# A two-layer decoder with top-2 experts on one core: sums of x kept in PSUM, two more weight slots, other load order

## Chip, cores, metric

One core of one Trainium2 chip. The metric is the device time of one execution in microseconds (us). The kernel before takes 749.85 us, the median of 3 runs (747.26 to 752.99).

## What is computed

Two decoder layers over 256 tokens of width 1024, in fp32, batch 1. The reference, cut to what matters here:

```python
for l in range(2):
    h = rms_norm(x, norm1_g[l])
    proj = h @ w_in[l]                       # 1024 x 3072
    o_da = diff_attention(...)               # 4 heads of 2 x 64
    o_sb = stick_breaking_attention(...)     # 8 heads of 64
    x = x + concat(norm(o_da), norm(o_sb)) @ w_out[l]
    h2 = rms_norm(x, norm2_g[l])
    # 32 experts in 4 groups: best group, then the best 2 of its 8 experts, with weights w
    hg = einsum('sd,edf->sef', h2, w_gate)   # every expert: 1024 x 256
    hu = einsum('sd,edf->sef', h2, w_up)     # 1024 x 256
    act = silu(hg) * hu * combine
    x = x + einsum('sef,efd->sd', act, w_down)   # 256 x 1024
```

Only the two chosen experts of a token count, so the kernel computes each expert on its own tokens alone. All weights are read once: 96 matrices of 1024 KB for the experts of a layer, and 16 such pieces for its two projections (12 of `w_in`, 4 of `w_out`).

## The kernel before

The five engines each run their own program, written out by hand, and meet by semaphores. One layer has three stretches. First comes attention: x is transposed (`transpose_x`, line 1162), projected block by block, the heads are computed, and `out_proj` adds to x. Then comes routing: the router's matmuls (`router`, L1304), a long row of small DVE operations that finds the experts, the ranks of tokens within an expert and the counts, and the selection matrices. `keep_clock` (L1311) issues matmuls whose result nobody reads.

Then come the experts, in 8 sets of 4 experts ("lanes"). A set gives each of its experts 32 slots for tokens; a fixed pair of sets comes first (sets 0 and 1), and the other six are sorted by how many tokens their fullest expert has. Where an expert has more than 32 tokens, the set makes further rounds (`more`, as against `first`). In this run the third set of each layer does. A set's work on PE, in order, is:

- `gate_or_up` twice (L1353): the gate and the up product, 4 experts side by side in the array, each reading its weights from slots of SBUF;
- `gather` of the *following* set (L1328): its tokens' normed x, picked by a matmul with a 0/1 matrix; then the transposition of its selection weights (`transpose_weights`, L1337);
- `transpose_act` (L1374), then `down` in two column halves (L1385), which ends with the signal that SP takes as `dn_used`;
- `scatter` (L1397): four matmuls that bring the rows back to tokens, into four banks of PSUM, from where DVE adds each to `x_sb` (`into_x`, L904).

Beside it ACT computes the exponential of the gate (L595) and copies half of y (L599); DVE finishes the activation (L876 to L887), copies it (L892), copies the other half of y (L896) and makes the following set's selection.

**Weights and slots.** SBUF holds 19 slots of 1024 KB for weights. Gates and ups use alternate slots by the parity of the set, but lane 3's up has a single slot (9) for both parities, and the four downs have one set of slots. So before routing ends, 19 matrices of a layer can be there: all 12 of set 0, and 4 gates and 3 ups of set 1. SP issues all loads into one queue, in program order, and an issue that waits holds back all behind it (`load_first_sets`, `load_further_sets`). For each set g from 1 to 7 the latter issues, in this order: up of lane 3 of set g once the ups of set g-1 are used; the four gates of g+1 once the gates of g-1 are used (`gate_used`, raised by ACT after its exponential, L612 and L625); the four downs of g once those of g-1 are used (`dn_used`, L638); three ups of g+1. For g = 1 the gates come ahead of the up. In set 7 the downs come as 8 half matrices, so that the first column half can start early. The numbers of the six sorted sets are read into registers in one go (L415), once the whole sort is done (`routed`).

PE reads a set's count (how full its fullest expert is) after `transpose_act` of the set before it, and for set 0 after it has waited for `routed`. The first set's gathered tokens are copied by DVE after the sort.

Of the kernel before, what the change touches and what calls it, by code (L numbers as in the profile page):

```python
# [24 lines left out]
ALU = mybir.AluOpType  # L25
# [3 lines left out]
P = 128  # L29
# [62 lines left out]
SC_BANK = [(4, 5), (6, 7)]  # L92
# [28 lines left out]
def decoder(nc, const, x, norm1_g, w_in, q_norm_g, k_norm_g, lambda_q1, lambda_k1, lambda_q2, lambda_k2,  # L121
            da_out_g, sb_out_g, w_out, norm2_g, w_router_group, b_router_group, w_router_expert,
            b_router_expert, w_gate, w_up, w_down, out):
    with ExitStack() as ctx:
# [9 lines left out]
        xn = sb("xn", [P, TT, D])  # L134
        hTbuf = sb("hTbuf", [P, KC * SEQ])
        qkT = sb("qkT", [P, 4 * PAIRS * SEQ])
        cst = sb("cst", [P, C_END])
        g1T = sb("g1T", [P, KC])
        g2T = sb("g2T", [P, KC])
        wr = sb("wr", [P, KC, GROUPS + EXPERTS])  # L140
# [50 lines left out]
        hT = hTbuf[:, :].rearrange("p (k t) -> p k t", k=KC)  # L191

        def slot(n):
            return wbuf[:, n * SLOT:(n + 1) * SLOT]
        stage = slot(SLOT_STAGE).rearrange("p (b t c) -> p b t c", b=2, t=TT)
# [5 lines left out]
        sp = [xn[:, w // 2, (w % 2) * HALF:(w % 2 + 1) * HALF] for w in range(4)] + \  # L202
# [8 lines left out]
        def take(n):  # L211
# [4 lines left out]
        eg, rg, tg = take(FF), take(FF), take(FF)  # L216
        act_sb = take(FF)
        actT = take(FF).rearrange("p (c s) -> p c s", c=FC)
        sel = take(TT * P).rearrange("p (t s) -> p t s", t=TT)
        selw = take(TT * P).rearrange("p (t s) -> p t s", t=TT)  # L220
        selwT2 = [take(TT * P).rearrange("p (t s) -> p t s", t=TT),
                  hTbuf[:, KC * P:KC * P + TT * P].rearrange("p (t s) -> p t s", t=TT)]
        hgT_more = hTbuf[:, 0:KC * P].rearrange("p (k s) -> p k s", k=KC)
        selwT_more, sel_more, selw_more = [hTbuf[:, (KC + n * TT) * P:(KC + (n + 1) * TT) * P]
                                           .rearrange("p (t s) -> p t s", t=TT) for n in (1, 2, 3)]

        y_more = hTbuf[:, 0:D]
        actT_more = hTbuf[:, (KC + 2 * TT) * P:(KC + 3 * TT) * P].rearrange("p (c s) -> p c s", c=FC)
        act_more = hTbuf[:, (KC + 3 * TT) * P:(KC + 4 * TT) * P]
# [4 lines left out]
        first_half, more_half = slice(0, FF), slice(FF, 2 * FF)  # L234
        SELW_BANK = 6
        FIRST_GATE, FIRST_UP, MORE_GU = 2, 3, 5
        FIRST_ACT, MORE_ACT = 7, 4
        FIRST_DN, MORE_DN = (4, 5), (2, 3)
# [11 lines left out]
        dn_in, last_dn_in = sem("dn_in"), sem("last_dn_in")  # L250
        out_done = sem("out_done")
# [18 lines left out]
        pos_ps, total_ps, routed = sem("pos_ps"), sem("total_ps"), sem("routed")  # L270

        STEPS = ["sel_ready", "selw_ready", "gathered0", "gathered1", "selwT_ps", "hg0", "hg1", "selwT_out", "gu_ps", "gate_exp",
                 "act_out", "actT_ps", "actT_out", "dn0_ps", "dn1_ps", "y_d", "y_a", "sc00_ps", "sc01_ps", "sc10_ps", "sc11_ps"]
        first = {n: sem(n) for n in STEPS}
        more = {n: sem("more_" + n) for n in STEPS}
        x_more, x_moe, x_tile = sem("x_more"), sem("x_moe"), [sem(f"x_tile{t}") for t in range(TT)]
# [16 lines left out]
        def params(l):  # L293
            yield dag[:, :], bcast(da_out_g[l], 2 * HD)
            yield sbg[:, :], bcast(sb_out_g[l], HD)
            yield g2T[:, :], norm2_g[l].rearrange("(p k) -> p k", k=KC)
            yield wr[:, :, 0:GROUPS], w_router_group[l].rearrange("(p k) n -> p k n", k=KC)
            yield wr[:, :, GROUPS:], w_router_expert[l].rearrange("(p k) n -> p k n", k=KC)
            yield br[:, 0:GROUPS], bcast(b_router_group[l], GROUPS)
            yield br[:, GROUPS:], bcast(b_router_expert[l], EXPERTS)  # L300
        N_PAR = 7 * 16
# [1255 lines left out]
```

## Time and profile before

| | |
|---|---|
| timed runs, median (range) | 749.85 us (747.26 to 752.99) |
| the profiled execution | 746.18 us |
| its span, first to last instruction | 744.4 us |
| mean granted TensorE clock | 0.956 |
| PE busy | 656.6 us (88%) |
| DVE, ACT busy | 309.4 us, 117.9 us |
| moved from and to HBM | 239.13 MB, 321 GB/s over the span |

The profile counts times in us from the first instruction. The experts' stretch of the first layer runs from about 167 to 378 us, that of the second from about 534 to 741 us. A busy share over the whole span mixes the stretches, so the readings below go by stretch.

### The profile page before, as it was taken

To read this page: it belongs to the slowest core of one execution; us is meant where nothing else is said; L and a number is where in the kernel's file an instruction comes from. 1 tells how busy PE (TensorE), PEld (TensorE's weight loads), DVE (VectorE), ACT (ScalarE), POOL (GpSimd) and SP (SyncE) were. 2 spreads that over 40 slices of the span, in tenths; PEclk is the share of its full clock that TensorE was granted. 3 is DMA by queue.
4 is the path that set the end of the run, shared out by engine and by line. 5 is a ranking of instruction groups with operands and counts; after the bars stand their busy time and mean duration, and the time that the engine had idled before them with its cause. 6 is when DMAs were issued, how large, how long until landed. Compare 5 with 4: busy or idle time off the path is not lost.

```text
span 744.4 us, 12442 instructions
## 1 busy us (share of the span) xinstructions
PE 656.6 (88%) x4804; PEld 379.6 (51%) x4805; DVE 309.4 (42%) x633; ACT 117.9 (16%) x288; POOL 8.5 (1%) x18
## 2 busy tenths in 40 slices
PE   7999999988798898775999999999888989885866
PEld 4478555475455354423344875555744545533522
DVE  0445664153334343422333476631634344422413
ACT  3103442220000000000031035313100000000000
POOL 0002000000000000000020000000000000000000
PEclk8999999999899999978999999999999999988979
DMA  8798436537999999999999631394299999999995
GB/s 312 257 355 280 168 113 273 227 123 284 381 422 395 392 424 421 421 421 423 383 360 390 278 144 66 114 390 163 77 397 421 422 422 421 422 422 421 422 402 222
DMA packets 52920, 239.13 MB, mean 321 GB/s; under 512 B 7761, under 2 KB 8049, under 8 KB 29329
## 3 DMA queue, kind: packets, MB, share of 16 engines
q1 hardware_dynamic: 52416, 238.16, 80.3%
q0 software_dynamic: 464, 0.47, 0.5%
q8 instruction: 23, 0.38, 0.2%
q14 instruction: 17, 0.13, 0.0%
HBM read 237.56 MB, written 1.05 MB: 321 GB/s over the span
## 4 chain that ended last, share of the span: by engine, by line
PE 67%; DMA 18%; DVE 6%; issue 5%; DVEq 2%; SPq 1%; ACT 1%; ACTq 0%
DMA wbuf<-in_w_down 17%; PE bank L1199 13%; PE bank L1385 11%; PE bank L1353 8%; PE bank L1189 7%; PE bank L1297 7%; PE bank L1397 6%; PE bank L1328 5%; PE bank L1364 2%; DMA wbuf<-in_w_in 1%; PE bank L1277 1%; SPq L366 1%; PE bank L1258 1%; PE bank L1304 1%; PE bank L1232 1%
## 5 line engine op out<-in xcount | busy, mean ns | idle before, releaser
L1199 PE MATMUL bank<-wbuf,hTbuf 128*128 128x512 f32 x256 | 115.8, 608 | 3.7 <-DMA wbuf<-in_w_in 3.4
L1385 PE MATMUL bank<-wbuf,qkT 128*32 128x512 f32 x512 | 71.6, 708 | 52.9 <-DMA wbuf<-in_w_down 45.7
L1353 PE MATMUL bank<-wbuf,qkT 128*32 128x256 f32 x2048 | 113.8, 380 | 2.2 <-DVE qkT L868 2.2
L1353 PEld LDWEIGHTS bank<-wbuf,qkT 128*32 128x32 f32 x2048 | 65.3, 110 | 54.2 <-issue 10.6
L1199 PEld LDWEIGHTS bank<-wbuf,hTbuf 128*128 128x128 f32 x256 | 48.8, 194 | 62.9 <-issue 59.2
L1328 PE MATMUL bank<-qkT,xn 128*128 128x128 f32 x512 | 64.6, 286 | 11.6 <-issue 10.7
L1328 PEld LDWEIGHTS bank<-qkT,xn 128*128 128x128 f32 x512 | 61.3, 199 | 18.9 <-issue 18.9
L904 DVE TENSOR_TENSOR x_sb<-x_sb,bank 128x512 f32<-128x512 f32 x72 | 49.5, 688 | 50.8 <-PE bank L1397 50.8
L1385 PEld LDWEIGHTS bank<-wbuf,qkT 128*32 128x32 f32 x512 | 17.2, 127 | 97.4 <-issue 90.4
L1189 PE MATMUL bank<-hTbuf,wbuf 128*128 128x256 f32 x256 | 56.5, 380 | 0.0
L1297 PE MATMUL bank<-wbuf,hTbuf 128*128 128x512 f32 x128 | 56.0, 593 | 0.0
L1189 PEld LDWEIGHTS bank<-hTbuf,wbuf 128*128 128x128 f32 x256 | 48.2, 190 | 7.0 <-issue 0.7
L896 DVE COPY qkT<-bank 128x512 f32<-128x512 f32 x16 | 11.1, 692 | 76.2 <-PE bank L1385 76.2
L1297 PEld LDWEIGHTS bank<-wbuf,hTbuf 128*128 128x128 f32 x128 | 23.9, 190 | 27.7 <-issue 27.7
L878 DVE RECIPROCAL qkT<-qkT 128x256 f32<-128x256 f32 x18 | 31.6, 1753 | 1.4
L1397 PE MATMUL bank<-qkT 128*128 128x512 f32 x64 | 30.1, 612 | 2.3 <-DVEq L957 2.3
L599 ACT COPY qkT<-bank 128x512 f32<-128x512 f32 x16 | 9.4, 586 | 132.9 <-PE bank L1385 132.9
L1397 PE MATMUL bank<-qkT,hTbuf 128*128 128x512 f32 x64 | 30.3, 616 | 0.0
L892 DVE COPY qkT<-bank 128x256 f32<-128x256 f32 x16 | 6.8, 424 | 55.6 <-PE bank L1374 55.6
L595 ACT ACTIVATE qkT<-bank 128x256 f32<-128x256 f32 x18 | 6.9, 385 | 127.0 <-PE bank L1353 113.2
L1397 PEld LDWEIGHTS bank<-qkT 128*128 128x128 f32 x64 | 11.0, 189 | 21.7 <-issue 17.9
L1041 DVE TENSOR_TENSOR x_sb<-x_sb,bank 128x512 f32<-128x512 f32 x8 | 5.5, 685 | 37.3 <-PE bank L1297 37.3
(219 smaller groups left out, 589.4 us busy)
## 6 DMA issues: line engine op xcount, KB each, us to landing
wbuf<-in_w_gate SPq DMA_DIRECT2D x64, 1024.0 KB, 14.3
wbuf<-in_w_up SPq DMA_DIRECT2D x64, 1024.0 KB, 17.9
wbuf<-in_w_down SPq DMA_DIRECT2D x56, 1024.0 KB, 13.4
wbuf<-in_w_in SPq DMA_DIRECT2D x24, 1024.0 KB, 14.6
wbuf<-in_w_out SPq DMA_DIRECT2D x8, 1024.0 KB, 6.4
wbuf<-in_w_down SPq DMA_DIRECT2D x16, 512.0 KB, 7.4
x_sb<-in_x SPq DMA_DIRECT2D x2, 512.0 KB, 5.9
out<-x_sb SPq DMA_DIRECT2D x2, 512.0 KB, 2.6
```

Source lines behind the costliest of these rows:

```text
L599: nc.scalar.copy(dst[:, HALF:], ps[bank][:, :]).then_inc(s["y_a"], 1)
L878: V.reciprocal(rg, rg)
L896: V.tensor_copy(dst[:, 0:HALF], ps[bank][:, :]).then_inc(s["y_d"], 1)
L904: last.append(V.tensor_tensor(x_sb[:, t, c], x_sb[:, t, c], ps[SC_BANK[t][h]][:, :], ALU.add))
L1189: last = MM(ps[PROJ_BANK[i][t]][:, a * SEQ:(a + 1) * SEQ], block_rows(i, k)[:, cols], hT[:, k, :], start=(k == 0), stop=(k == KC - 1))
L1199: last = MM(ps[PROJ_BANK[i][t]][:, :], hT[:, k, t * P:(t + 1) * P], block_rows(i, k), start=(k == 0), stop=(k == KC - 1))
L1297: last = MM(ps[OP_BANK[t][h]][:, :], hT[:, k, t * P:(t + 1) * P], block_rows(i, k), start=(k == 0), stop=(k == KC - 1))
L1328: last = MM(ps[k // 4][:, (k % 4) * P:(k % 4 + 1) * P], xn[:, t, k * P:(k + 1) * P], sel[:, t, :], start=(t == 0), stop=(t == TT - 1))
L1353: last = MM(ps[bank][j * SLOTS:(j + 1) * SLOTS, 0:FF], hgT[:, k, j * SLOTS:(j + 1) * SLOTS], halves[:, at[j], k, :], start=(k == 0), stop= ...
L1364: last = MM(ps[MORE_GU][j * SLOTS:(j + 1) * SLOTS, :].rearrange("p (a f) -> p a f", a=2), hgT_more[:, k, j * SLOTS:(j + 1) * SLOTS], halve ...
L1385: last = MM(ps[banks[h]][j * SLOTS:(j + 1) * SLOTS, :], src[:, c, j * SLOTS:(j + 1) * SLOTS], at[j][:, c * D + h * HALF:c * D + (h + 1) * ...
L1397: MM(ps[SC_BANK[t][h]][:, :], weights[:, t, :], src[:, h * HALF:(h + 1) * HALF], start=True, stop=True).then_inc(s[f"sc{t}{h}_ps"], 1)
```

## The change

It does six things.

1. **Slots.** The buffers `xn` (normed x and attention output) and `hTbuf` (x transposed) become two more weight slots, 19 (`SLOT_XN`) and 20 (`SLOT_HT`). Lane 3's up of odd sets goes to slot 19, lane 0's down of odd sets to slot 20. So 21 matrices are loaded ahead: `up(1,3)` after the attention output is transposed, and `down(1,0)` after the router's matmuls.
2. **Load order.** For g from 1 to 7 SP now issues: four gates of g+1, four ups of g+1, downs of lanes 1 to 3 of g, down of lane 0 of g+1. Set 7 has 6 half matrices at the end.
3. **x in PSUM.** After the router, `keep_x` writes x by four matmuls with the identity into banks 4 to 7; every scatter adds to them there, and x is copied out once at the end of the layer, three quarters by DVE and one by ACT. `into_x` goes. The normed x, which the gathers read, is written by ACT to a scratch tile and then, by a second copy (`normed_to_x`), in place of x.
4. **Order within a set.** With four banks taken, downs of both kinds share banks 2 and 3. The selection weights of a set are transposed after its own ups, no longer ahead of its downs. In the last set the scatters of the first column half stand between the two halves of the downs.
5. **Counts and numbers.** SP reads each set's number just ahead of its gates. PE reads the count of the next set after the ups of a set; for set 0 it waits for `first_counts`, an earlier signal than `routed`. ACT raises `gate_used` ahead of its exponential. DVE copies the first half of set 0's gathered tokens before the sort, and ACT the second.
6. **Router by column halves.** The router's rows and the transposes of x for it go by column halves, so that a half can be transposed when its half of x is there.

```diff
-SLOTS_W = 19
-SLOT_STAGE, SLOT_VALUES, SLOT_SCRATCH = 13, 14, 15
+SLOTS_W = 21
+SLOT_STAGE, SLOT_VALUES, SLOT_SCRATCH, SLOT_XN, SLOT_HT = 13, 14, 15, 19, 20
-UP_SLOT = [[4, 5, SLOT_STAGE, 9], [6, 7, 8, 9]]
-DOWN_SLOT = [10, 11, SLOT_VALUES, 16]
+UP_SLOT = [[4, 5, SLOT_STAGE, 9], [6, 7, 8, SLOT_XN]]
+DOWN_SLOT = [[10, 11, SLOT_VALUES, 16], [SLOT_HT, 11, SLOT_VALUES, 16]]
...
+                sp_.wait_ge(oT_ps, l * 4 + 4)
+                load_up(l, 1, 3)
                 sp_.wait_ge(oproj_ps, l * 4 + 3)
                 load_gate(l, 1, 3)
...
+                sp_.wait_ge(lg_ps, (l + 1) * TT)
+                load_down(l, 1, 0)
 
             def load_further_sets(l):
                 sp_.wait_ge(routed, l + 1)
-                for g in range(2, SETS):
-                    at = SETS - g
-                    kept = sp_.value_load(which[0:1, at:at + 1], min_val=int(BIG) - SETS + 1, max_val=int(BIG) - 2)
-                    set_at[g] = sp_.snap(int(BIG) - kept)
                 for g in range(1, SETS):
-
-                    if g > 1:
-                        sp_.wait_ge(up_used, l * SETS + g)
-                        load_up(l, g, LANES - 1)
                     if g + 1 < SETS:
+                        at = SETS - (g + 1)
+                        kept = sp_.value_load(which[0:1, at:at + 1], min_val=int(BIG) - SETS + 1, max_val=int(BIG) - 2)
+                        set_at[g + 1] = sp_.snap(int(BIG) - kept)
                         sp_.wait_ge(gate_used, l * SETS + g)
                         for j in range(LANES):
                             load_gate(l, g + 1, j)
-                    if g == 1:
                         sp_.wait_ge(up_used, l * SETS + g)
-                        load_up(l, g, LANES - 1)
+                        for j in range(LANES):
+                            load_up(l, g + 1, j)
                     sp_.wait_ge(dn_used, l * SETS + g)
                     if g + 1 < SETS:
-                        for j in range(LANES):
+                        for j in range(1, LANES):
                             load_down(l, g, j)
-                        for j in range(LANES - 1):
-                            load_up(l, g + 1, j)
+                        load_down(l, g + 1, 0)
                     else:
                         for h in range(2):
-                            for j in range(LANES):
+                            for j in range(1, LANES):
                                 load_down_half(l, g, j, h)
...
+            def normed_to_x(l, t):
+
+                act.wait_ge(x_kept, l * TT + t + 1)
+                nc.scalar.copy(xn[:, t, :, :], xn_first[t]).then_inc(xn_ready, 1)
...
+                with act.If(most <= SLOTS):
+                    act.wait_ge(first["gu_ps"], act.snap(n * LANES))
+                    act.sem_inc(gate_used, 1)
                 gate(first, n, FIRST_GATE)
-
                 with act.If(most <= SLOTS):
-                    act.sem_inc(gate_used, 1)
                     act.wait_ge(up_ps, act.snap(n * LANES))
                     act.sem_inc(up_used, 1)
+                weights_copy(first, n, selwT, SELW_BANK)
...
-                for t, add in enumerate(into_x(first, n)):
-                    add.then_inc(x_tile[t], 1)
-                gap().then_inc(x_moe, 1)
...
+                for t, h in ((0, 0), (1, 0), (0, 1)):
+                    dve.wait_ge(x_ps[t][h], l + 1)
+                    V.tensor_copy(x_sb[:, t, h * HALF:(h + 1) * HALF], ps[X_BANK[t][h]][:, :]).then_inc(x_tile[t], 1)
...
+            def keep_x(t):
+
+                for h in range(2):
+                    last = MM(ps[X_BANK[t][h]][:, :], ident, x_sb[:, t, h * HALF:(h + 1) * HALF], start=True, stop=False)
+                last.then_inc(x_kept, 1)
...
+            def downs_and_scatters(s, n, parity, src, weights, second_half, last=False):
+
                 pe.wait_ge(s["actT_out"], n)
...
+                pe.wait_ge(s["selwT_out"], n)
+                down(s, n, parity, src, 0)
+                if last:
+                    scatter(s, n, weights, 0, last)
+                down(s, n, parity, src, 1, second_half)
+                if not last:
+                    scatter(s, n, weights, 0, last)
+                scatter(s, n, weights, 1, last)
...
                 gate_or_up(n, FIRST_UP, UP_SLOT[parity], up_ps)
+
+                pe.wait_ge(routed, l + 1)
+                pe.reg_mov(count, pe.value_load(cnt[0:1, bass.ds(SETS - 1 - g, 1)], min_val=0, max_val=SEQ))
+                transpose_weights(first, n, SELW_BANK)
```

Where instructions move, at three places. The first is the end of SP's queue of expert loads, from the last gate of set 7 to the first issue group of set 7's halves. Before:

```order
L359 ISA
L359 DMA wbuf<-in_w_gate 128x2048
L366 DMA wbuf<-in_w_down 128x2048 [waits dn_used]
L366 DMA wbuf<-in_w_down 128x2048 x3
L363 DMA wbuf<-in_w_up 128x2048 x3
L363 DMA wbuf<-in_w_up 128x2048 [waits up_used]
L370 DMA wbuf<-in_w_down 128x2x512 [waits dn_used]
L370 DMA wbuf<-in_w_down 128x2x512 x3
```

And now, from the same gate on:

```order
L362 ISA
L362 DMA wbuf<-in_w_gate 128x2048
L366 DMA wbuf<-in_w_up 128x2048 [waits up_used]
L366 DMA wbuf<-in_w_up 128x2048 x3
L370 DMA wbuf<-in_w_down 128x2048 [waits dn_used]
L370 DMA wbuf<-in_w_down 128x2048 x3
L375 DMA wbuf<-in_w_down 128x2x512 [waits dn_used]
L375 DMA wbuf<-in_w_down 128x2x512 x2
```

The four ups of set 7 moved from behind the downs of set 6 to ahead of them; behind those three downs there is now one down of set 7, and then the halves.

The second is PE within an even set, from the gather of the following set to the point ahead of the downs. Before (`actT` in `qkT`, the `cst` operand is the identity):

```order
L1325 REGISTER_ALU
L1328 MATMUL bank<-qkT,xn 128x128 [waits sel_ready]
L1328 MATMUL bank<-qkT,xn 128x128 x15
L1337 MATMUL bank<-cst,qkT 128x128 [waits selw_ready,selwT_out,x_moe]
L1337 MATMUL bank<-cst,qkT 128x128
L1374 MATMUL bank<-cst,qkT 128x128 [waits act_out]
L1374 MATMUL bank<-cst,qkT 128x128
L1446 ISA
L1446 TENSOR_LOAD sorted_i
L1446 ISA x3
L1448 COMPARE_AND_BRANCH [waits dn_in]
```

Now the same reading of the count (`TENSOR_LOAD`) and the transposition of the weights (L1365) follow the last up matmuls (L1381):

```order
L1381 MATMUL bank<-wbuf,qkT 32x256 x15
L1473 ISA [waits routed]
L1473 TENSOR_LOAD sorted_i
L1473 ISA x2
L1365 MATMUL bank<-cst,qkT 128x128 [waits selw_ready]
L1365 MATMUL bank<-cst,qkT 128x128
L1475 COMPARE_AND_BRANCH
```

The reading moved from ahead of the downs to between the ups and the gather, where PE's next matmuls stand behind it.

The third is PE in the last set, the downs (L1385, now L1411) and what follows. Before:

```order
L1385 MATMUL bank<-wbuf,qkT 32x512 [waits actT_out]
L1385 MATMUL bank<-wbuf,qkT 32x512 x7
L1382 ISA
L1385 MATMUL bank<-wbuf,qkT 32x512 [waits last_dn_in]
L1385 MATMUL bank<-wbuf,qkT 32x512 x7
L1453 COMPARE_AND_BRANCH
```

Now, with the scatters (L1419) in between and behind:

```order
L1411 MATMUL bank<-wbuf,qkT 32x512 [waits selwT_out,actT_out]
L1411 MATMUL bank<-wbuf,qkT 32x512 x7
L1419 MATMUL bank<-qkT 128x512 [waits y_d]
L1419 MATMUL bank<-qkT 128x512
L1411 MATMUL bank<-wbuf,qkT 32x512 [waits last_dn_in]
L1411 MATMUL bank<-wbuf,qkT 32x512 x7
L1419 MATMUL bank<-qkT 128x512 [waits y_a]
L1419 MATMUL bank<-qkT 128x512
```

Each pair of scatters now stands directly behind the half of the downs whose result it needs.

## Rows read from the trace of the kernel before

**Rows 1.** The page: DMA busy tenths and GB/s in 40 slices of 18.6 us.

```profile
DMA  8798436537999999999999631394299999999995
GB/s 312 257 355 280 168 113 273 227 123 284 381 422 395 392 424 421 421 421 423 383 360 390 278 144 66 114 390 163 77 397 421 422 422 421 422 422 421 422 402 222
```

**Rows 2.** Chain that ended last: start us, us, what.

```profile
328.87 22.05 DMA wbuf<-in_w_down
350.91 0.30 issue
351.21 6.37 PE bank L1385 x32
357.58 3.72 PE bank L1397 x8
361.30 7.17 PE bank L1353 x128
...
370.50 3.85 PE bank L1385 x32
374.35 3.72 PE bank L1397 x8
378.07 0.90 PE bank L1162 x8
...
714.54 5.62 PE bank L1385 x32
```

**Rows 3.** Timeline of SP's DMA issues, 165 to 380 and 530 to 745 us.

```profile
171.17 2.40 SPq L359 DMA_DIRECT2D wbuf<-in_w_gate  x4
...
235.37 2.41 SPq L359 DMA_DIRECT2D wbuf<-in_w_gate  x4
...
538.06 2.63 SPq L359 DMA_DIRECT2D wbuf<-in_w_gate  x4
...
595.88 1.91 SPq L359 DMA_DIRECT2D wbuf<-in_w_gate  x4
```

**Rows 4.** Stretches: us, busy by engine, PEclk, DMA share, GB/s.

```profile
185.00:190.00 5.00, 5.00 (x24) 1.63 (x20) 2.43 (x5) 0.59 (x1) 0.00 (x0) 1.00 0.57 210
190.00:230.00 40.00, 34.44 (x394) 21.18 (x390) 16.18 (x30) 2.10 (x5) 0.00 (x0) 0.91 1.01 422
235.00:240.00 5.00, 4.49 (x38) 4.25 (x38) 3.52 (x6) 0.37 (x1) 0.00 (x0) 1.00 0.86 331
245.00:250.00 5.00, 4.08 (x37) 1.21 (x30) 0.69 (x1) 1.17 (x2) 0.00 (x0) 1.00 0.82 341
555.00:715.00 160.00, 127.39 (x1328) 69.29 (x1324) 61.73 (x107) 8.82 (x20) 0.00 (x0) 0.94 1.01 422
```

**Rows 5.** Timeline, end of routing and set 0 of the first layer.

```profile
165.46 0.17 DVE L1148 CAST sorted_i<-ev 128x12 int32<-128x12 f32 x1
...
166.97 5.39 PE L1353 MATMUL bank<-wbuf,qkT 128*32 128x256 f32 x96 [1.18 <-DVE qkT L868]
...
170.77 0.38 ACT L595 ACTIVATE qkT<-bank 128x256 f32<-128x256 f32 x1 [4.57 <-PE bank L1353]
```

**Rows 6.** Timeline, last set of the second layer.

```profile
731.82 0.41 PE L1374 MATMUL bank<-cst,qkT 128*128 128x128 f32 x2 [0.89 <-DVE qkT L887]
732.26 0.42 DVE L892 COPY qkT<-bank 128x256 f32<-128x256 f32 x1 [0.59 <-PE bank L1374]
...
733.23 3.64 PE L1385 MATMUL bank<-wbuf,qkT 128*32 128x512 f32 x32 [1.00 <-DVE qkT L892]
...
735.29 0.69 DVE L896 COPY qkT<-bank 128x512 f32<-128x512 f32 x1 [2.61 <-PE bank L1385]
...
737.10 0.59 ACT L599 COPY qkT<-bank 128x512 f32<-128x512 f32 x1 [9.10 <-PE bank L1385]
```

**Rows 7.** Timeline of set 1, first layer: PE's gather behind the ups.

```profile
201.86 6.07 PE L1328 MATMUL bank<-qkT,xn 128*128 128x128 f32 x32 [4.98 <-issue]
```

More of the change, by code:

```diff
@@ L250, in decoder @@
         dn_in, last_dn_in = sem("dn_in"), sem("last_dn_in")
+        dn0_in = [sem(f"dn0_in{p}") for p in range(2)]
         out_done = sem("out_done")
@@ L587, in oT_half, with weights_copy, first_gathering @@
                                ps[OT_BANK[t][1]][:, :].rearrange("p (k c) -> p k c", k=4)).then_inc(oT_a, 1)
-            def weights_copy(s, n, dst, half):
+            def weights_copy(s, n, dst, bank):
                 act.wait_ge(s["selwT_ps"], n)
-                nc.scalar.copy(dst.rearrange("p t s -> p (t s)"), ps[SELW_BANK][:, half]).then_inc(s["selwT_out"], 1)
+                nc.scalar.copy(dst.rearrange("p t s -> p (t s)"), ps[bank][:, 0:TT * P]).then_inc(s["selwT_out"], 1)
+            def first_gathering(l):
+                act.wait_ge(first["gathered1"], l * SETS + 1)
+                for k in range(4, 8):
+                    last = nc.scalar.activation(hgT[:, k, :], ps[1][:, (k - 4) * P:(k - 3) * P], ACT.Copy,
+                                                scale=g2T[:, k:k + 1])
+                last.then_inc(first["hg1"], 1)
             def gate(s, n, bank):
@@ L952, in expert_set @@
                     act_copy(more, m, ps[MORE_ACT][:, 0:FF], actT_more)
[L953 to L964 removed]
+                    y_copy(more, m)
+                y_copy(first, n)
+            V.memset(xa[:, 0, 0:P], 0.0).then_inc(zeros_ready, 1)
             V.memset(cnt[:, 0:1], 0)
@@ L1164, in transpose_x, with transpose_half @@
                         last.then_inc(hT_ps, 1)
+            def transpose_half(t, h):
+                for k in range(KC // 2):
+                    last = TR(ps[2 * t + h][:, k * P:(k + 1) * P], x_halves[:, t, h, k, :], ident)
+                last.then_inc(hT_ps, 1)
             def block_rows(i, k):
@@ L1390, in scatter, with down @@
-            def scatter(s, n, weights, src):
-                pe.wait_ge(s["selwT_out"], n)
-                pe.wait_ge(s["y_d"], n)
-                for t in range(TT):
-                    for h in range(2):
-                        if t == 0 and h == 1:
-                            pe.wait_ge(s["y_a"], n)
-                        MM(ps[SC_BANK[t][h]][:, :], weights[:, t, :], src[:, h * HALF:(h + 1) * HALF],
-                           start=True, stop=True).then_inc(s[f"sc{t}{h}_ps"], 1)
+            def down(s, n, parity, src, h, second_half=None):
+                if h == 1 and second_half is not None:
+                    pe.wait_ge(last_dn_in, second_half)
+                at = [slot(DOWN_SLOT[parity][j]) for j in range(LANES)]
+                for c in range(FC):
+                    for j in range(LANES):
+                        last = MM(ps[DN_BANK[h]][j * SLOTS:(j + 1) * SLOTS, :], src[:, c, j * SLOTS:(j + 1) * SLOTS],
+                                  at[j][:, c * D + h * HALF:c * D + (h + 1) * HALF], start=(c == 0), stop=(c == FC - 1))
+                        if c == FC - 1:
+                            last.then_inc(s[f"dn{h}_ps"], 1)
@@ new lines, in scatter @@
+            def scatter(s, n, weights, h, last):
+                pe.wait_ge(s["y_a" if h else "y_d"], n)
+                for t in range(TT):
+                    mm = MM(ps[X_BANK[t][h]][:, :], weights[:, t, :], y[:, h * HALF:(h + 1) * HALF], start=False, stop=last)
+                    if last:
+                        mm.then_inc(x_ps[t][h], 1)
+            def downs_and_scatters(s, n, parity, src, weights, second_half, last=False):
+                pe.wait_ge(s["actT_out"], n)
+                pe.wait_ge(s["selwT_out"], n)
+                down(s, n, parity, src, 0)
+                if last:
+                    scatter(s, n, weights, 0, last)
[3 more added lines that the diff above has]
+                scatter(s, n, weights, 1, last)
@@ L1527, in _ @@
                 router(l, 1, 1)
-                keep_clock(12)
+                for t in range(TT):
+                    keep_x(t)
                 ranks(l)
```

295 lines of the change are left out of this document (138 added, 157 removed).

## Prediction

> **What bounds the kernel now.** I read four views, in this order. First the page's row of DMA use [rows 1]: in slices 11 to 20 and 29 to 38 the queues run at nines and near 422 GB/s, and these are the experts' stretches; in attention they run at 1 to 7 tenths. So only the experts' stretch is bound by transfers, and only a change in what must be moved there, or when it may start, can gain.
>
> Second, the chain that ended last [rows 2]. It is to show which transfer is late. In the first layer it runs over "DMA wbuf<-in_w_down" again and again: PE waits for the downs of its set. The last such wait is that of set 6: they land at 350.91 us. From there on the chain is PE's own: downs 6.37, scatters 3.72, gate and up of set 7 from 361.30, its downs at 370.50, its scatters to 378.07. That is 27.2 us in which no transfer is late by a microsecond. So a layer ends 27.2 us after set 6's downs have landed, and everything turns on when they land. In the second layer PE starts them at 714.54.
>
> Third, SP's issues [rows 3], which say when the queue may start: the first gates that need a used slot are issued at 171.17 and 538.06.
>
> Fourth, the rate [rows 4]: 422 GB/s over 40 us and over 160 us. A matrix of 1024 KB is 1.049 MB, so it takes 2.485 us. The check: 96 matrices a layer, 19 there beforehand, and 8 issued behind set 6's downs (4 ups and 4 downs of set 7) leave 69 that must have passed: 171.5 us. 171.17 + 171.5 = 342.7, and 4.5 us were lost with the queue dry: 5 us at 210 instead of 422 GB/s (2.5), at 331 (1.1) and at 341 (0.9) [rows 4]. That makes 347.2; they landed at 350.91, so 3.7 go to the start and the end of the pipeline. In the second layer 538.06 + 171.5 = 709.6 against some 714.2, so 4.6. The account holds within 1 us in both layers.
>
> **Part 1, slots and load order.** 21 matrices are there beforehand, two more. But the four ups of set 7 now stand ahead of set 6's downs in SP's queue, and only four downs stand behind them. So 96 - 21 - 4 = 71 must pass, against 69. Set 6's downs land 2 x 2.485 = 5.0 us later in each layer, all else equal. The total moved falls, but not what lies ahead of the transfer that is waited for. What was gained is that set 7's weights come early, and PE cannot use this, since in its program set 7 follows set 6's downs. This term is the surest; its bounds are 4.5 and 5.5.
>
> **Part 2, when the queue may start.** ACT releases the gates' slots before its exponential, which took 0.38 [rows 5], and PE's first gate can start a little earlier: it began at 166.97, 1.34 after the sort's last write had begun and ended at 165.63 [rows 5], and this wait for the sort is gone. But PE has just ended its gather there and must still read a count, so I give only 0.2. The four matmuls of `keep_x` are as long as four scatters, 3.72 us [rows 2], and take the place of filler matmuls while DVE sorts; the two extra copies on ACT lie beside the same sort. Sum: 0.6 us earlier per layer. Bounds: 0, and 2.0 if the whole 1.34 is gained and the hiding is perfect.
>
> **Part 3, a dry queue.** Set 2 has a further round in this run, so the slots of its gates are released late: the next gates were issued at 235.37 and 595.88 [rows 3]. Ahead of them in the new queue stand gates and ups of sets 2 and 3, downs 1 to 3 of sets 1 and 2 and down 0 of sets 2 and 3: 8+3+1+8+3+1 = 24 matrices, 59.6 us. With about 1.1 us from an issue to the first bytes (my share of the 3.7) the queue is empty in the first layer at 170.6 + 1.1 + 59.6 = 231.3, in the second at 598.2.
>
> The release itself moves. PE's read of a count stood ahead of the downs, where PE waited anyway; now the gather is behind it. Its price no row shows alone. In the last set the transposes start at 731.82 and the downs at 733.23, 0.55 after DVE's copy has ended [rows 6]; the read and two branches lie in these 1.41. So the bounds are 0 (PE's instruction stream runs ahead and hides it) and 1.34. I take 0.6 a set, near the 0.55. The three sets 0 to 2 make 1.8, the second transposition ahead of the further round 0.4, the earlier start takes 0.25 off: 1.95 later. So the gates of set 4 come at 237.3 + 1.1 = 238.4, and the queue is dry for 7.1 us in the first layer, where 4.5 were lost before: +2.6. In the second they come at 598.9, 0.7 us dry, none before: +0.7. Bounds: 0 to +5 and 0 to +3. The Trainium skill gives a floor of about 600 ns for such a load (DMA: Bandwidth & Descriptors, "Latency and other measured facts"), which no run here shows by itself; with it the sum would stay as it is.
>
> What goes: DVE's additions to x (0.69 us each) no longer stand behind the scatters. In sets 0 to 6 nothing waited for them on the chain [rows 2], so I cost this at nothing; its cover is PE's own gate and up. In the further round of set 2 the scatters of both rounds follow their downs one by one. That moves `dn_used` of set 2 some 5 us later, but by then 8 gates and ups are queued, 19.9 us of transfers. Hidden; without this cover it would cost those 5 us once per layer.
>
> **Part 4, the tail.** In the last set the scatter of the first half stands directly behind the first half of the downs. DVE's copy of y takes 0.69 and started 0.24 after half of the 3.64 us of downs [rows 6], so PE waits about 1.0; ACT's copy takes 0.59 and the second scatter waits about 0.9. Before, the other half of the downs covered the first, the first scatters the second. +1.9 per layer. Bounds: 0.9, if a transfer would have held PE there anyway, and 2.5. At the layer's end x is copied from PSUM where it was added before; 0.2 in the first layer, 0.3 in the second, where the output's last transfer waits for it.
>
> **Router by halves, SP's numbers one by one.** PE's work is the same and it was never idle there; SP's first read is done before the gates are used. Zero, within 0.3.
>
> **The sum.** First layer 5.0 - 0.6 + 2.6 + 1.9 + 0.2 = 9.1; second 5.0 - 0.6 + 0.7 + 1.9 + 0.3 = 7.3; together 16.4 us. The profiled execution took 746.18 us, 1.8 more than its span and 3.7 below the median of the timed ones, 749.85. The sum gives 762.6 on the one and 766.2 on the other; I take the middle, 764 us.
>
> **Rivals.** *The bytes decide* (faster). If a layer's end follows the last byte moved, two matrices less per layer and 0.6 us save 2 x 5.6 = 11.2 us: 739. For it: nines in the row of DMA use. Against it: in the last set no transfer was late by a microsecond, and the transfers ended before PE did [rows 2]. It would decide only if PE's 27.2 us after set 6's downs fell below the time of what is left to move, 4 matrices, 10 us. The Trainium skill's rule speaks for it: issue the DMA early and wait on its semaphore late (DMA: Bandwidth & Descriptors, "Rules for kernel authors"). By that rule the earlier ups of set 7 gain; the trace disagrees, since they delay the downs in front of which PE stands. Chance 0.08.
>
> *The start moves far more* (about no change). If routing ends 4 us earlier in each layer, because DVE and ACT no longer finish the sort ahead of the first gates and no queue runs dry, then 16.4 - 2 x 3.4 - 3.3 = 6.3, and with a tail that costs half, 4.4: 754. Against it: the gather ended only shortly before 166.97. Chance 0.14.
>
> *Code fetch* (slower still). PE stood 4.98 us for nothing visible where it first passed the long code of the further rounds [rows 7]. The new program is longer and the last set has its own copy of downs and scatters, run for the first time at the layer's end, on the chain. Two such stalls: 764 + 10 = 774. For it: the gap is there. Against: in later sets there is none. Chance 0.12.
>
> **How the numbers follow.** My forecast has 0.66. About 1% is what a measurement of this kernel tells from no change; 1% over 749.85 is 757.3. Faster: the first rival and a little of the second, 0.10. Within 1%: the rest of the second and the low end of mine, 0.13. Slower: 0.77. All low ends together give 746.2 + 5 = 751, all high ends 775. The range goes to 749 at the lower end, to take in most of the second rival, and to 773 at the upper.
>
> **What would show it.** Right: the downs of set 6 land 6 to 8 us later against the layer's start in the first layer and 4 to 6 in the second; the chain after them has two gaps of about 1 us between downs and scatters of set 7; the DMA rate drops to near zero for some microseconds around 231 us; the first gates are issued about 0.6 us earlier. Wrong: set 6's downs at the old time or earlier, a chain that ends in transfers, or first gates earlier by over 2 us. If PE's gather starts directly behind the ups, the read of the count is hidden and part 3 is too large.

## The result, and the profile after

The changed kernel takes 773.56 us (median of 4 runs, 771.12 to 775.74), the kernel before 749.95 beside it (747.26 to 752.99): ratio 1.0348, 95% interval 1.0315 to 1.0381. It is slower, by 23.6 us. I had forecast 764 and a range up to 773: the direction was right, the size too small by 9.6 us.

The page of the changed kernel, its granted TensorE clock and DMA use in 40 slices of 19.3 us, and the row of the queue of instruction fetches:

```profile
PEclk9999999999999978978989999999998999987979
DMA  8798229549996999996899333286499999999953
GB/s 311 238 376 303 93 108 392 225 174 418 419 388 243 422 415 418 419 415 288 294 383 317 109 129 144 108 338 227 177 405 417 421 391 418 421 422 423 421 219 133
...
q8 instruction: 50, 0.82, 0.5%
```

Against [rows 1] there is now a hole in the first layer's stretch of experts (243 GB/s in the slice from 232 us), and the row of instruction fetches, q8, has 50 packets of 16 KB. Before it had 23:

```profile
q8 instruction: 23, 0.38, 0.2%
```

The chain of waits of the changed kernel, first layer (start us, us, what). It answers to [rows 2]:

```profile
195.03 1.70 PE bank L1356 x14
196.73 3.79 issue
200.52 3.80 PE bank L1356 x18
...
212.32 5.37 issue
217.69 8.86 PE bank L1381 x126
...
285.84 5.98 issue
291.82 9.18 PE bank L1381 x128
...
363.80 5.34 PE bank L1411 x32
...
380.57 6.40 issue
...
399.31 1.10 PE bank L1174 x8
```

The downs of set 6 start at 363.80, 12.6 us after those of before, and the layer's end (the first transposes of the next layer) is at 399.31 against 378.07 [rows 2]: 21.2 later, where my sum had 9.1. Between 399.31 and the span's end at 773.8 lie 374.5 us, against 366.3 before: 8.2 later, where my sum had 7.3. So the second layer came out near the sum, and nearly the whole surplus is in the first. There the chain shows what the second doesn't have: waits for nothing visible ("issue") of 3.6 to 6.4 us, in the middle of a run of matmuls, in pass after pass of PE's loop. Of the gate and up products behind such a stop, the 7.04 us row becomes 8.86 and 9.18.

The same as a view of PE's waits (what PE waited for: us in total, times, longest), changed kernel:

```profile
PE bank L1411 <- DMA wbuf<-in_w_down: 33.1, 5, 9.9
PE bank L1356 <- issue: 18.0, 10, 3.8
PE bank L1381 <- issue: 16.7, 3, 6.0
PE bank L1411 <- issue: 12.1, 5, 2.8
PE bank L1402 <- issue: 6.8, 1, 6.8
```

Those "issue" rows make 53.6 us; before, all such rows of this view together made 15.9 us (10.7 of them in front of the gather). And the fetches fall where the stops are: in the stretch from 240 to 402 us, the last three quarters of the first layer's loop, the view of DMA use counts 23 packets,

```profile
q8 instruction: 23, 0.38, 1.1%
```

while in the second layer from 600 to 774 us there are none, and before there were none from 240 to 360 us either. Both layers run the same code, written out twice.

### The profile page after: what moved, and what is told of

Read it like the earlier page. It is cut to its first block, busy times and chain, and to the rows that moved or that the text cites. A ratio compares the mean times of both kernels' runs of the same rounds, so it can differ in the third digit from the quotient of the medians.

```text
span 773.8 us, 12265 instructions
## 1 busy us (share of the span) xinstructions
PE 668.7 (86%) x4772; PEld 383.3 (50%) x4773; DVE 262.1 (34%) x565; ACT 124.9 (16%) x302; POOL 10.4 (1%) x21
## 4 chain that ended last, share of the span: by engine, by line
PE 69%; DMA 16%; issue 7%; DVE 3%; SPq 2%; ACT 1%; DVEq 1%; ACTq 0%
DMA wbuf<-in_w_down 14%; PE bank L1217 11%; PE bank L1411 11%; PE bank L1381 11%; PE bank L1207 7%; PE bank L1315 7%; PE bank L1356 7%; PE bank L1419 6%; PE bank L1392 2%; DMA lamv<-in_lambda_k 2%; PE bank L1295 1%; PE bank L1323 1%; PE bank L1276 1%; PE bank L1250 1%; SPq L464 1%
## 5 line engine op out<-in xcount | busy, mean ns | idle before, releaser
L1381 PE MATMUL bank<-wbuf,qkT 128*32 128x256 f32 x2048 | 119.9, 393 | 16.7 <-issue 16.7
L1217 PE MATMUL bank<-wbuf 128*128 128x512 f32 x256 | 114.5, 603 | 3.5 <-DMA wbuf<-in_w_in 3.0
L1411 PE MATMUL bank<-wbuf,qkT 128*32 128x512 f32 x512 | 73.0, 718 | 43.2 <-DMA wbuf<-in_w_down 33.1
L1381 PEld LDWEIGHTS bank<-wbuf,qkT 128*32 128x32 f32 x2048 | 67.6, 114 | 72.4 <-issue 33.9
L1356 PE MATMUL bank<-qkT,x_sb 128*128 128x128 f32 x576 | 73.6, 288 | 19.0 <-issue 18.0
L1356 PEld LDWEIGHTS bank<-qkT,x_sb 128*128 128x128 f32 x576 | 70.0, 201 | 23.1 <-issue 22.7
L1217 PEld LDWEIGHTS bank<-wbuf 128*128 128x128 f32 x256 | 48.4, 193 | 62.0 <-issue 58.7
L1419 PE MATMUL bank<-qkT 128*128 128x512 f32 x128 | 59.7, 607 | 3.5 <-DVE qkT L916 1.8
L1411 PEld LDWEIGHTS bank<-wbuf,qkT 128*32 128x32 f32 x512 | 18.7, 128 | 86.7 <-issue 81.7
L1207 PE MATMUL bank<-wbuf 128*128 128x256 f32 x256 | 56.5, 380 | 0.0
L1315 PE MATMUL bank<-wbuf 128*128 128x512 f32 x128 | 56.0, 593 | 0.0
L1207 PEld LDWEIGHTS bank<-wbuf 128*128 128x128 f32 x256 | 48.2, 190 | 7.0 <-issue 0.7
L1419 PEld LDWEIGHTS bank<-qkT 128*128 128x128 f32 x128 | 22.8, 189 | 42.2 <-issue 26.7
L1315 PEld LDWEIGHTS bank<-wbuf 128*128 128x128 f32 x128 | 23.9, 190 | 27.7 <-issue 27.7
L885 DVE TENSOR_TENSOR qkT<-bank,g2T 128x512 f32<-128x512 f32 x34 | 22.1, 683 | 6.8 <-PE bank L1356 6.6
L573 ACT ACTIVATE wbuf<-wbuf,dmax 128x128 f32<-128x128 f32 (+1 forms) x32 | 14.1, 442 | 33.0 <-DVE dmax L797 32.8
## 6 DMA issues: line engine op xcount, KB each, us to landing
wbuf<-in_w_gate SPq DMA_DIRECT2D x64, 1024.0 KB, 12.7
```

The lines of the kernel that those rows point to most:

```text
L573: last = nc.scalar.activation(s, s, ACT.Exp, bias=dmax[:, u, c:c + 1], accum_out=dsum[:, u, c:c + 1])
L885: V.tensor_tensor(hgT[:, 4 * h:4 * h + 4, :], ps[h][:, :].rearrange("p (k s) -> p k s", k=4), g2T[:, 4 * h:4 * h + 4].unsqueeze(2).broadca ...
L1207: last = MM(ps[PROJ_BANK[i][t]][:, a * SEQ:(a + 1) * SEQ], block_rows(i, k)[:, cols], hT[:, k, :], start=(k == 0), stop=(k == KC - 1))
L1217: last = MM(ps[PROJ_BANK[i][t]][:, :], hT[:, k, t * P:(t + 1) * P], block_rows(i, k), start=(k == 0), stop=(k == KC - 1))
L1315: last = MM(ps[OP_BANK[t][h]][:, :], hT[:, k, t * P:(t + 1) * P], block_rows(i, k), start=(k == 0), stop=(k == KC - 1))
L1356: last = MM(ps[k // 4][:, (k % 4) * P:(k % 4 + 1) * P], xn[:, t, k, :], sel[:, t, :], start=(t == 0), stop=(t == TT - 1))
```

## The experiments

```
                    layer 0's loop      layer 1's loop      lengths
before              1377 to 3017        4356 to 5997        1641, 1642
after               1341 to 3048        4351 to 6059        1708, 1709
```

A loop of about 1641 or 1708 instructions touches 7 or 8 blocks, as it happens to lie. If the stream has 24 to 54 instructions ahead of this list, layer 0's loop of the changed kernel touches 8 and the three others 7. Theory A: PE's store holds a loop over 7 blocks and not one over 8, and then fetches it again in each of the four turns. Theory B: the surplus comes from slots, load order and the dry queue. To move a loop without touching anything else, PE jumps over matmuls that never run. The edit, with its two numbers in matmuls:

```diff
+            unused = counter(pe, "pe_unused")
+            def skipped(n):
+                with pe.If(pe.snap(unused) > 0):
+                    keep_clock(n)
+            skipped(50)
...
             for l in range(DEPTH):
+                if l == 1:
+                    skipped(11)
```

**e1_after_shifted**: the changed kernel with skipped(50) and skipped(11). Expected:

> The changed kernel, with PE instructions that are jumped over and never run: 200 at the start of PE's program and 44 ahead of layer 1 (and a few for the jumps). Nothing else moves; only where PE's two expert loops lie in its instruction stream. Counted in blocks of 256 instructions (16 KB, the size of each instruction packet in the trace), layer 0's loop then touches 7 blocks instead of 8, layer 1's 7 as before. Theory A (the surplus of layer 0, 21.4 us where my sum had 9.1, is code fetched again in every pass, because a loop over 8 blocks isn't held): instruction packets fall from 50 to about 23, PE's stalls on nothing visible go from every pass of layer 0, and the time falls by 10 to 14 us, to about 761. Theory B (the surplus comes from the slots, the load order and the dry queue): packets may change, the time stays at 773.6 within 1.

Measured: 753.78 us (749.83 to 757.97), before 748.42 beside it: ratio 1.0068 (1.0044 to 1.0093). 19.8 us are gone (21 by the two ratios), more than the 10 to 14 expected. Its rows of the page and of PE's waits:

```profile
q8 instruction: 24, 0.39, 0.2%
...
PE bank L1411 <- DMA wbuf<-in_w_down: 60.4, 8, 10.1
PE bank L1411 <- issue: 9.3, 4, 2.6
PE bank L1356 <- issue: 6.0, 6, 1.9
```

Theory A holds, B falls. The account between the two profiles: stops on "issue" 53.6 against 15.3 (+38.3), waits for downs 33.1 against 60.4 (-27.3), PE busy 668.7 against 661.0 (+7.7, the slower matmuls behind the stops): +18.7, and the spans differ by 773.8 - 756.2 = 17.6. So a stop costs what is left once the wait for a transfer that it shortens is taken off, and the slower matmuls behind it.

**e2_after_both_over**: the changed kernel, with skipped(24) ahead of layer 1 alone.

> The changed kernel with 96 jumped-over PE instructions ahead of layer 1 alone, so that layer 1's loop touches 8 blocks as well. Theory A: about 27 more instruction packets (some 77 in all), stalls in every pass of layer 1 too, and 10 to 14 us more: about 786. Theory B: 773.6 within 1.

Measured: 801.89 us (798.95 to 805.6), ratio 1.0711 (1.065 to 1.0771): 28.3 more than the changed kernel, twice the expected price of 10 to 14.

```profile
q8 instruction: 78, 1.28, 0.7%
...
PE bank L1356 <- issue: 43.7, 16, 6.2
PE bank L1381 <- issue: 34.2, 9, 5.9
```

28 packets more. There is no wait for downs left at all in this view; the whole price of the last stops shows.

**e3_before_over**: the kernel before, with skipped(14) at the start.

> The kernel before with 56 jumped-over PE instructions at the start of PE's program, so that layer 0's loop, with 1641 instructions shorter than the changed kernel's 1708, touches 8 blocks instead of 7; layer 1's stays at 7. Theory A: packets rise from 23 to about 50, PE stalls in each pass of layer 0, and the time rises by 8 to 14 us, to about 760. Theory B, and any theory in which the length of the code or the changed kernel's own order matters and not the place: 750 within 1.

Measured: 783.8 us (780.47 to 784.32), ratio 1.0469 (1.0408 to 1.053). 50 packets, as expected; the price is 35 us, not 8 to 14:

```profile
q8 instruction: 50, 0.82, 0.4%
...
PE bank L1328 <- issue: 31.6, 9, 5.6
PE bank L1385 <- DMA wbuf<-in_w_down: 23.7, 3, 9.8
PE bank L1353 <- issue: 22.1, 6, 4.3
```

So the kernel before carries the same trap, and had only escaped it by its place.

**e4_shifted_old_tail**: skipped(49) and skipped(12), which put both loops where e1 has them, and

```diff
                 down(s, n, parity, src, 0)
-                if last:
-                    scatter(s, n, weights, 0, last)
                 down(s, n, parity, src, 1, second_half)
-                if not last:
-                    scatter(s, n, weights, 0, last)
+                scatter(s, n, weights, 0, last)
```

> As e1_after_shifted (7 blocks for both loops), and in the last set of a layer the scatter of the first half stands behind both halves of the downs again, as before the change. My sum's part 4 has 1.9 us per layer for that order: 3.8 us less than e1_after_shifted, the two gaps of about 0.9 us behind the last downs gone. If the end of a layer is set by something else than PE (a transfer of the next layer's weights, say), 0 to 1.9.

Measured: 750.02 us (747.1 to 755.21), ratio 1.0024 (0.9998 to 1.005): 3.76 less than e1 (10 runs of each; the difference is known to about 2 us), against 3.8 in my sum.

**e5_before_inside**: the kernel before, with skipped(57) at the start.

> The kernel before with 228 jumped-over PE instructions at the start of PE's program: both expert loops move in the instruction stream and both still touch 7 blocks of 256 instructions. Theory A (the cost is in touching an eighth block): packets stay at 23 or 24 and the time at 748 within 1.5, though the padding is four times as long as in e3_before_over, which cost 35 us. Rival (any move, or any jump over many instructions, costs): 10 us or more. It is also a second profile of the kernel before beside which the others can be laid.

Measured: 744.54 us (743.7 to 747.02), ratio 0.9954 (0.993 to 0.9977), before 748.95 beside it. No cost for the jump, 24 packets, but 4.4 us *faster*, which I had not expected. SP's timeline shows where: the gates of set 4 are issued at 231.97 instead of 235.37 [rows 3], with the first ones at 171.82 instead of 171.17.

```profile
171.82 2.40 SPq L359 DMA_DIRECT2D wbuf<-in_w_gate  x4
...
231.97 1.91 SPq L359 DMA_DIRECT2D wbuf<-in_w_gate  x4
```

The stops of the loop's first turn (4.98 us in [rows 7]) fell elsewhere (3.93 us in this chain), set 2's release came 4 us earlier after the first one, and the queue did not run dry as long: in the stretches from 185, 235 and 245 us it has 369, 421 and 360 GB/s where [rows 4] has 210, 331 and 341.

**e6_ups_last_behind**: e4, and in `load_further_sets`

```diff
-                        for j in range(LANES):
+                        ahead = 0 if g == SETS - 2 else LANES
+                        for j in range(ahead):
                             load_up(l, g + 1, j)
                     sp_.wait_ge(dn_used, l * SETS + g)
                     if g + 1 < SETS:
                         for j in range(1, LANES):
                             load_down(l, g, j)
+                        for j in range(ahead, LANES):
+                            load_up(l, g + 1, j)
                         load_down(l, g + 1, 0)
```

> As e4_shifted_old_tail, and SP issues the four ups of the last set behind downs 1 to 3 of the set before it, instead of ahead of them. By part 1 of my sum the downs of set 6 then stand behind 67 matrices instead of 71: 4 x 2.485 = 9.9 us earlier, where PE can take them (it is ready some 9 us earlier); the last set's weights land just before PE gets to them. So 8 to 9.5 us less per layer: 750.0 - 17 = 733, range 730 to 737, faster than the kernel before. If instead the bytes decide (the last transfer, whatever the order), no change within 2.

Measured: 731.48 us (728.45 to 734.18), ratio 0.9757 (0.9704 to 0.981). 18.5 us less than e4, 20.0 by the two ratios: the two matrices of part 1 and two more per layer, at their price (8 x 2.485 = 19.9). In the chain of its first layer set 6's downs stand at 346.17, and the wait for the transfer in front of them is gone:

```profile
334.44 7.04 PE bank L1384 x128
341.86 3.57 PE bank L1359 x32
345.69 0.44 DVE qkT L915
346.17 3.76 PE bank L1414 x32
...
353.57 11.56 DMA wbuf<-in_w_down
365.18 1.92 PE bank L1414 x16
```

Now the layer ends with a transfer, the second halves of the last downs, for which PE waits 1.01 us in the first layer. The same holds for e5, the kernel before at another place, whose chain has its last downs behind a transfer in both layers:

```profile
370.58 1.92 PE L1385 MATMUL bank<-wbuf,qkT 128*32 128x512 f32 x16 [1.07 <-DMA wbuf<-in_w_down]
```

(e5's timeline, first layer.) So at a good place of the loop PE's own chain and the last byte are within about 1 us of each other in both programs, and either can come last.

**e7_ups_behind_from5** (`ahead = 0 if g > 3 else LANES`) and **e8_downs1_earlier** (`ahead = 2 if g == 1 else 0 if g > 3 else LANES`), both otherwise as e6.

> As e6_ups_last_behind, but the ups of each of sets 5, 6 and 7 (g > 3) stand behind the downs of the set before them. Set 6's downs stand behind the same 67 matrices, so they land at the same time; PE only comes to its waits earlier and waits longer there. Expected 733, within 2 of e6_ups_last_behind; if PE rather than the queue set the pace between sets 5 and 6, up to 3 less; if the longer waits cost clock, up to 4 more.

> As e7_ups_behind_from5, and two of set 2's ups stand behind set 1's downs instead of ahead of them. In layer 1 of e1_after_shifted PE waited for set 1's downs and came to set 2 about 4.1 us later than in the kernel before, so the gates of set 4 were issued later and the queue ran dry for some 2.7 us. With the downs 5 us earlier that goes: 2 to 3 us less in layer 1, 0 to 2 in layer 0: 2 to 5 less than e7_ups_behind_from5. If set 2's ups are then late for PE, or the queue is dry before set 4 anyway, no change.

Measured: 732.56 us (730.59 to 734.44), ratio 0.9786 (0.9741 to 0.9831), as expected; and 731.42 us (729.41 to 732.07), ratio 0.9754 (0.9711 to 0.9797), 1.1 less where I had expected 2 to 5, inside the spread. There was little left to gain: in e7 the stretches in which the queue ran dry have 357 GB/s (from 230 us) and 382 (from 585), a loss of 0.8 and 0.5 us, and in e8 the same stretches have 421 and 424. The chains of e7 and e11 end with PE's own work in both layers, that of e8 with a transfer in the first layer alone, 0.48 us late.

**e9_new_tail_again**, **e10_reordered_unshifted** and **e11_best_again**, on one chip. e9 is e8 with the changed kernel's tail; e10 is e8 without the skipped matmuls, so that layer 0's loop touches 8 blocks; e11 is the kernel of e8.

> As e8_downs1_earlier, with the changed kernel's own tail (in the last set the first scatter between the halves of the downs). In e1 against e4 that tail cost 3.8 us, because the downs of the last set were long there. Now in e6_ups_last_behind layer 1 ends on the transfer of the second halves (its chain has them at 710.03 to 720.85, only 16 matmuls left behind them), so the first scatter would run while PE waits anyway. If such a transfer holds PE in both layers: 0 to 2 us less than e8. If PE's own chain sets the end, as e8_downs1_earlier's chain shows (downs 718.54, 3.64 without a gap): 2 to 3.8 more, as before: 731.4 + 3 = 734. I expect the second.

> e8_downs1_earlier without the jumped-over instructions: the changed kernel with the new order of the loads and the old tail, and its loop of layer 0 touching 8 blocks again. If code fetch and the load order are separate costs: layer 0 stalls in each pass, about 50 instruction packets, and 15 to 25 us more than e8: about 751, no faster than the kernel before, so that the gain of the order would not have been seen. If the earlier transfers hide the stalls (PE waits there anyway): 5 or less more.

> The kernel of e8_downs1_earlier once more, beside e9 and e10 on the same chip: 731.4 within 1.5, ratio 0.975 to 0.979 to the kernel before.

Measured, with 746.88 us for the kernel before: e9 736.15 us (732.88 to 738.25), ratio 0.985 (0.9818 to 0.9882); e10 759.92 us (755.19 to 763.7), ratio 1.016 (1.0127 to 1.0192); e11 731.91 us (728.64 to 733.63), ratio 0.9788 (0.9756 to 0.982). The tail costs 4.2 here, close to e1 against e4 and a little above the 2 to 3.8 expected. The place of the loop costs 28.0, above the 15 to 25 expected, with 50 packets against 24: unshifted, the better order would have looked like a loss.

e11 beats both kernels: 15.0 us below the one before, some 42 below the changed one. It is the change with its tail undone, 14 loads of each layer in another order, and some 61 matmuls of dead code in the right places. Most of the gain is already in e6, which moves 4 loads of each layer.

## Why the prediction was wrong

**The result, by the sum.** On top of what I had summed came a cost that I had priced as a rival at 10 us and 0.12: code fetch. That rival gave 774, which is the time that came out, but not for its reasons: I had it as two stops, on first use of new code. It was a whole loop fetched again in every turn, at 19.8 us (e1 against the changed kernel). The step that failed is the sentence against it, "in later sets there is none". The row of the kernel before could not say that: its loop lay in 7 blocks, and the change added 67 instructions to it and moved it (by 36 towards the front, which alone would have kept it within 7). What I could have done is to count: the length of the loop and its place were to be had before any run, and the rows of q8 (23 packets, none in the later turns) showed that at most some 7 blocks were known to be held. The Trainium skill says that PE's instruction store has 128 KiB, 2048 instructions, refilled in blocks of 256, and that for a long kernel that streams through it crossing a block is "mostly hidden" (Runtime: NRT & Kernel Launch, "Instruction fetch mechanics"). The size fits these runs if one of its eight blocks is the one being filled, which is argued, not shown; "mostly hidden" does not hold for a loop that touches eight blocks: most of its stops are 3.6 to 6.4 us each.

Without that cost the sum was too large. e1 stands 5.1 us above the kernel before by its ratio, and 8.6 above e5, the kernel before at an equally good place (1.0068 / 0.9954 = 1.0114). I had 16.4. Term by term:

**Part 1, 71 matrices instead of 69: right.** From the first gates' issue to set 6's downs, e1's first layer takes 352.53 - 171.04 = 181.5 us, e5's 348.20 - 171.82 = 176.4: 5.1 more, predicted 5.0. In the second layer it is 723.55 - 540.48 = 183.1 against 712.30 - 536.14 = 176.2, 6.9 more; about 1.6 of that is the dry queue of part 3. e6 takes four matrices off the queue ahead and gets 18.5 us for both layers, predicted 17.

```profile
171.04 2.40 SPq L362 DMA_DIRECT2D wbuf<-in_w_gate  x4
...
232.14 2.04 SPq L362 DMA_DIRECT2D wbuf<-in_w_gate  x4
...
352.53 5.91 PE bank L1411 x32
```

(SP's timeline and the last row from the chain, e1.)

**Part 2, when the queue may start: two effects that I had not separated.** In the changed kernel the first gates are issued at 168.62 and 557.74. The first is 2.55 us earlier than before, over the 2 us that I had named as a sign of being wrong. From the end of layer 0 (399.31) to the second are 158.4 us, before 538.06 - 378.07 = 160.0 [rows 2, 3]: 1.6 earlier, against my 0.6. In e1 neither layer shows it (171.04, and 540.48 - 380.38 = 160.1).

In the first layer e1 had lost the time at the start of the program: its second run of 32 projection matmuls starts at 29.12, that of the changed kernel at 26.72 and that of before at 27.57. From there to the first gates it takes 141.9 us in e1 and in the changed kernel, and 143.6 before, so the gain is 1.7 in both. In the second layer the difference between the two runs lies in the matmuls of `keep_x`, first the changed kernel, then e1, with e1's stretch:

```profile
543.24 3.68 PE L1335 MATMUL bank<-x_sb,cst 128*128 128x512 f32 x8
...
524.31 5.38 PE L1335 MATMUL bank<-x_sb,cst 128*128 128x512 f32 x8
...
524.00:526.00 2.00, 2.00 (x7) 1.04 (x7) 1.17 (x8) 0.56 (x1) 0.00 (x0) 0.60 0.98 406
```

The same eight matmuls took 3.68 us at a granted clock of 1.00, the upper of its two levels (2.4 GHz), and 5.38 where it had fallen to 0.60, near the lower one (1.2 GHz); in e4 they took 6.54 at 0.50. In all three the router's 24 matmuls had run just before them, so what brings the clock down stays open. Of the ten profiles of the new program, six have 3.68 us for these matmuls and 158.4 from layer end to gates, two have 160.1, and two (e4, e11) 161.8. So the gain is 1.6 to 1.7 with the clock up and is lost again in `keep_x` with it down; on average over the ten it is 0.6, my figure, by luck: I had taken `keep_x` as hidden at its 3.72 us.

**Part 3, the dry queue: near in the changed kernel by luck, wrong at a good place of the loop.** The changed kernel's timeline of SP and its stretches:

```profile
168.62 2.10 SPq L362 DMA_DIRECT2D wbuf<-in_w_gate  x4
...
238.82 2.04 SPq L362 DMA_DIRECT2D wbuf<-in_w_gate  x4
...
620.09 2.08 SPq L362 DMA_DIRECT2D wbuf<-in_w_gate  x4
```

```profile
230.00:235.00 5.00, 5.00 (x48) 2.29 (x51) 0.75 (x2) 0.38 (x1) 0.00 (x0) 1.00 0.21 87
235.00:240.00 5.00, 4.16 (x39) 1.61 (x32) 1.03 (x2) 0.38 (x1) 0.00 (x0) 1.00 0.09 13
...
620.00:625.00 5.00, 4.27 (x36) 4.04 (x36) 3.59 (x6) 0.13 (x1) 0.00 (x0) 1.00 0.82 305
```

At 87 and 13 instead of 422 GB/s, 4.0 and 4.8 us are lost, at 305 another 1.4. Predicted were 7.1 and 0.7, near 231 us. But most of the first came from the stops: in e1 the gates of set 4 are issued at 232.14 and the stretch from 230 to 235 us still has 354 GB/s, a loss of 0.8. So at a good place the first layer's term is 0.8 - 4.5 = -3.7, not +2.6: the 4.5 us that the kernel before loses there come mostly with its own first-turn stops, of which e5 sheds 3.1 too. I took them as given. The price of the read was too large as well: in e1 the ups of set 0 end at 174.04, the two transpositions of the weights take 0.37 and the gather starts at 174.41, directly behind. That was my own sign that the read is hidden.

In the second layer I missed a step: set 1's downs stand behind 8 matrices of set 2 instead of 5, as set 6's do behind two more, and PE comes later to set 2. From the first gate product of set 0 to that of set 2 it takes 583.18 - 536.38 = 46.8 us in e1 and 574.46 - 531.95 = 42.5 in e5. The gates of set 4 are then issued at 602.77, 2.7 after 24 matrices had passed since 540.48, and the stretch from 600 us has 283 GB/s, a loss of 1.6. e8 takes part of the 4.3 back (567.09 - 522.96 = 44.1).

**Part 4, the tail: right.** Predicted 1.9 per layer; 3.76 for both in e1 against e4, 4.2 in e9 against e11. The two gaps stand in the chain of the changed kernel's last set: the scatters wait for DVE's copy and then for ACT's. They are 0.76 and 0.74 us, less than my 1.0 and 0.9; the rest is that downs and scatters take longer in halves (2.05 + 1.98 and 1.98 + 2.00, before 3.64 and 3.73).

```profile
759.99 2.05 PE bank L1411 x16
762.06 0.70 DVE qkT L916
762.80 1.98 PE bank L1419 x4
764.79 1.98 PE bank L1411 x16
766.87 0.59 ACT qkT L617
767.51 2.00 PE bank L1419 x4
```

**Laid end to end.** The profile of e1 against that of before: first gates 0.13 earlier; from there to set 6's downs +1.45 (5.0 of part 1, -3.7 of the dry queue); to the layer's end +0.99 (1.9 of the tail, and 0.9 less ahead of it); to the next gates +0.11; to set 6's downs +6.59 (5.0, and 1.6 of the dry queue); to the span's end +2.79. That makes 11.80, and the spans differ by 756.2 - 744.4 = 11.8. So with both loops in 7 blocks the term that was mis-sized is the dry queue of the first layer: +2.6 in my sum, -3.7 in e1. The medians differ by 5 only because e1's profiled execution is the slowest of its ten (757.97 against a median of 753.78) and that of before lies 2.2 below the median of 748.42 beside e1. The forecast was laid over one such execution, and this alone is worth 2 to 4 us.

**The rivals.** "The bytes decide" fell for the changed kernel. In e6, when the last set's ups no longer stood ahead of the downs, the last transfer was 1.0 us late, and in e5 1.1; the queue and PE's chain run nearly even there. "The start moves far more" fell: 1.7 and 1.6 us with the clock up, not 4.

## What to carry to other kernels

Where PE runs a long loop, count its instructions and the blocks that it touches before reading anything else out of a change: here an eighth block of 256 cost 20 to 35 us per loop of four turns, and moving the loop by jumped-over code took it back. The sign is the number of instruction packets beside stops on "issue" within a run of matmuls, in every turn. And where a queue is the bound, a slot more gains only if the load that is waited for next stands first in it: the same 21 slots gave +5 us per layer in one order and let e6 go below the kernel before in the other.

## What the runs showed that I had not expected

- A jumped-over stretch of 14 matmuls at the start of the program made the kernel before 35 us slower (e3), and one of 57 made it 4 us faster (e5).
- The price of the refetching depends on what is left to hide it: e3 against e5, stops 60.3 against 10.7 us, waits for downs 23.7 against 45.8, PE busy 669.4 against 656.7, which makes 40.2 (49.6 - 22.1 + 12.7) for spans that differ by 40.1.
- Gate and up products that take 7.04 us at a granted clock of 1.00 (187 to 194 us) take 8.86 and 9.18 behind a stop of over 5 us, where it is 0.66 (217 to 222 us) and 0.51 (292 to 296); over the whole span it is 0.945 in the changed kernel, 0.927 in e2 and 0.962 in e11.
- How many instructions lie ahead of the program's own list was fitted (24 to 54, if nothing else is put in) from the first two kernels; the runs that followed agree with it, but none narrows it.
